# Retention layer of a two-block model: the heads' norm four at a time, and the logarithms of the decays moved into an earlier stage

## The reference

```python
def retention_mixer(...):
    q, k, v, g = split(h @ w_in)         # q, k turned by rope for the latents
    logg = log_sigmoid(decay_logit)      # (2 directions, 8 heads)
    # per head and direction: S_t = exp(logg) * S_{t-1} + k_t v_t^T, y_t = q_t S_t
    y = y_forward + y_backward
    mu, var = mean(y), mean((y - mu)**2) # over the 128 channels of a head
    y = (y - mu) * rsqrt(var + EPS) * gn_g * silu(g)
    return y @ w_out
```

## Time and profile before

| | |
|---|---|
| median of 3 runs | 2895.98 us |
| lowest and highest run | 2881.82, 2899.46 us |
| the profiled execution, its own time | 2883.46 us |
| its span | 2881.5 us |
| busy: TensorE, VectorE, ScalarE | 90%, 42%, 14% of the span |
| products of q | 1309.1 to 1359 us of the span |
| attention stage | 1417.7 to 1565.4 us |
| of that, 1431.5 to 1550: TensorE, VectorE, ScalarE busy | 104.0, 81.9, 45.2 of 118.5 us |
| output projection | from 1565.85 us |

### The profile page before, as it was taken

The page is one execution under the profiler, slowest core; times in us unless marked ns, Lnnn a source line. Parts: engine busy times, 40 slices in busy tenths (PEclk is TensorE's granted clock), DMA queues, the critical chain, the costliest instruction groups (busy, mean ns, idle before and its releaser), DMA issues. The chain is left out here.

```text
span 2881.5 us, 53069 instructions
## 1 busy us (share of the span) xinstructions
PE 2580.2 (90%) x23771; PEld 1817.1 (63%) x23771; DVE 1200.3 (42%) x2046; ACT 417.2 (14%) x925; POOL 240.2 (8%) x219
## 2 busy tenths in 40 slices
PE   7999889589999998999788688888879988899999
PEld 3575675377787564588534564444438666788888
DVE  4635565511111113435767622223235655534452
ACT  2101350200000001100232200000010342110000
POOL 0000000122232210001100110000000300000000
PEclk9999879799999999999899899999999998999999
DMA  7331313689999993215243489999963200222211
GB/s 302 132 127 57 92 34 132 252 330 402 403 400 398 403 404 155 82 44 144 89 139 103 197 350 418 418 418 418 418 279 132 81 15 1 103 88 88 105 68 62
DMA packets 111482, 596.51 MB, mean 207 GB/s; under 512 B 13104, under 2 KB 35568, under 8 KB 47640
## 3 DMA queue, kind: packets, MB, share of 16 engines
q1 hardware_dynamic: 95880, 560.14, 49.2%
q0 software_dynamic: 12000, 22.48, 3.1%
q10 hardware_dynamic: 3376, 10.49, 0.9%
HBM read 572.77 MB, written 16.10 MB: 204 GB/s over the span
## 5 line engine op out<-in xcount | busy, mean ns | idle before, releaser
L1194 PE MATMUL moe_ps<-moe_ring,moe_xs 128*32 128x256 f32 x10240 | 595.9, 382 | 77.1 <-DMA moe_ring<-in_experts 59.8
L1194 PEld LDWEIGHTS moe_ps<-moe_ring,moe_xs 128*32 128x32 f32 x10240 | 393.3, 110 | 278.3 <-DMA moe_ring<-in_experts 83.7
L1194 PE MATMUL moe_ps<-moe_ring,moe_hid_t 128*32 128x256 f32 x5120 | 292.1, 380 | 13.5 <-DMA moe_ring<-in_experts 12.6
L1194 PEld LDWEIGHTS moe_ps<-moe_ring,moe_hid_t 128*32 128x32 f32 x5120 | 193.3, 110 | 113.0 <-DMA moe_ring<-in_experts 25.3
L1433 DVE TENSOR_TENSOR moe_hid<-moe_silu,moe_ps 128x512 f32<-128x512 f32 x32 | 22.0, 688 | 408.1 <-PE moe_ps L1194 398.4
L1394 DVE SCALAR_TENSOR_TENSOR x_feat<-moe_ps,mod,x_feat 128x512 f32<-128x512 f32 (+1 forms) x160 | 104.7, 718 | 122.0 <-PE moe_ps L1268 121.8
L1347 ACT ACTIVATE moe_silu<-moe_ps 128x512 f32<-128x512 f32 x32 | 19.1, 597 | 786.0 <-PE moe_ps L1194 786.0
L1457 DVE TENSOR_SCALAR moe_y<-moe_ps,moe_gates 128x256 f32<-128x256 f32 x42 | 17.8, 478 | 263.7 <-PE moe_ps L1194 263.7
L1225 POOL DMA_INDIRECT moe_rows<-h_rows,moe_rows_id x80 | 77.8, 972 | 476.6 <-DVE moe_xs L1414 363.0
L1235 POOL DMA_INDIRECT acc<-moe_y,moe_rows_id x42 | 66.6, 1586 | 346.0 <-DVE moe_y L1457 337.5
L649 PE MATMUL ffg_ps<-h_feat,feed_f_slots 128*128 128x256 f32 x352 | 82.1, 386 | 1.4 <-DVE h_feat L852 0.9
(11 more groups left out here) (690 smaller groups left out, 3911.7 us busy)
## 6 DMA issues: line engine op xcount, KB each, us to landing
moe_ring<-in_experts SPq DMA_DIRECT2D x384, 1024.0 KB, 27.8
x_feat<-in_ada_w SPq DMA_DIRECT2D x16, 1024.0 KB, 5.3
feed_f_slots<-in_ffn_gate SPq DMA_DIRECT2D x11, 1024.0 KB, 4.9
feed_f_slots<-in_ffn_up SPq DMA_DIRECT2D x11, 1024.0 KB, 5.0
feed_f_slots<-in_ffn_down SPq DMA_DIRECT2D x8, 1408.0 KB, 5.8
gate_rows<-in_ada_w SPq DMA_DIRECT2D x9, 1024.0 KB
qk_ada_w<-in_ada_w SPq DMA_DIRECT2D x8, 1024.0 KB, 4.9
mout_ada_w<-in_ada_w SPq DMA_DIRECT2D x8, 1024.0 KB, 4.7
```

The source lines that it names most:

```text
L1194: mm = pe.matmul(group_ps(part, g)[32 * q:32 * q + 32], turned[:, k * GROUP:(k + 1) * GROUP], ring[:, n % SLOTS, m, q * QUARTER:(q + 1) * ...
```

## The change

`logg` and its helpers move out of the attention stage: the operations on VectorE become `beside["vector"]` of the products of q, the Exp becomes ScalarE's work at the end of its first item. The attention stage waits for the three latent tables first and for the two context tables in head 0 behind its Exp. Two constant tables that the hybrid block also uses are loaded besides: `spread` (64 KB), of which `[:, 2]` has 1/128 in column 0 and zeros in 31 columns, and `back` (192 KB), of which `[:, 0]` has ones in rows 0, 32, 64 and 96.

The squares of four heads are kept in room of `K.h`. In round 5 (and behind the last mix) four products put the means of four heads on rows 0, 32, 64 and 96 of one bank; one root and one reciprocal serve the four heads; for each head a product with `back` spreads its row over all partitions, and VectorE multiplies y by that bank. The spreads of heads 0 to 3 stand before and behind the mixes of rounds 6 and 7, those of heads 4 to 7 at the end, in the four banks `ps_s`.

```diff
--- before.py
+++ after.py
@@ -2158,10 +2158,19 @@
         seven(nc, K, dram, "rv", feed, K.h, halves, evacuate_v, make=False, by_token=True)
 
         latents = K.h[:, :, 0:LAT]
+        logg, la, lb, lc = (sb(n, [P, 16]) for n in ("logg", "la", "lb", "lc"))
+
+        def decays_on_scalar(act, sig, c):
+            if c == 0:
+                log_sigmoid_on_scalar(act, sig, "g", la[:])
+
+        def decays_on_vector(dve, sig):
+            log_sigmoid_on_vector(dve, Steps(dve, sig["logg"]), sig, "g", K.cols("decay_logit", 16), la[:], lb[:], lc[:], logg[:])
+
         with ExitStack() as sub:
             rope = Rope(nc, sub, dram, v)
             seven(nc, K, dram, "rq", feed, latents, tails(K), add_into(q), after=rope.turn_k(k),
-                  beside={"gpsimd": rope.load_k(k)})
+                  beside={"gpsimd": rope.load_k(k), "scalar": decays_on_scalar, "vector": decays_on_vector})
             first, others = silu_behind(g, LAT)
             seven(nc, K, dram, "rg", feed, latents, tails(K), add_into(g), make=False, on_scalar=first, after=rope.turn_q(q),
                   beside={"gpsimd": rope.load_q(q), "scalar": others}, limit=feed.first[4] + 2)
@@ -2176,11 +2185,13 @@
                 tables.append(idle[:, at:at + width])
                 at += width
             later, sooner, once, ctx_f, ctx_b = tables
-            logg, la, lb, lc = (sbs(n, [P, 16]) for n in ("logg", "la", "lb", "lc"))
             lat_w, ctx_w = sbs("lat_w", [P, NL]), sbs("ctx_w", [P, NC])
             ctx_x = sbs("ctx_x", [P, NC])
             prob = sbs("prob", [P, 2, TT, LAT])
-            sq, rstd = sbs("sq", [P, LAT]), sbs("rstd", [P, LAT])
+            rstd = sbs("rstd", [P, LAT])
+            sq = lambda h: K.h[:, 2 * (h % 4):2 * (h % 4) + 2, LAT:TOK]
+            means, back, table = sbs("means", [P, 4, 32]), sbs("back", [P, 3, P]), sbs("table", [P, 1])
+            group = lambda h: slice(32 * (h % 4), 32 * (h % 4) + 32)
             ps_s = sub.enter_context(nc.psum_tensor("ret_pss", [P, 4, 512], F32))
             ps_y = sub.enter_context(nc.psum_tensor("ret_psy", [P, 2, 512], F32))
             ps_n = sub.enter_context(nc.psum_tensor("ret_psn", [P, 512], F32))
@@ -2191,7 +2202,9 @@
                 @block.sync
                 def _(sp):
                     for t, n in ((later, "later"), (sooner, "sooner"), (once, "once"), (ctx_f, "ctx_f"), (ctx_b, "ctx_b")):
-                        sp.dma_start(t, dram[n]).then_inc(sig["tables"], 16)
+                        sp.dma_start(t, dram[n]).then_inc(sig["ctx_tables" if n[0] == "c" else "lat_tables"], 16)
+                    for t, n in ((means, "spread"), (back, "back")):
+                        sp.dma_start(t[:], dram[n]).then_inc(sig["norm_tables"], 16)
                     for m in range(2 * HEADS):
                         side.load(sp, m)
 
@@ -2206,17 +2219,26 @@
                                            start=(j == 0), stop=(j == TT - 1))
                         mm.then_inc(sig["mixed"], 1)
 
-                    def sum_squares(h):
-                        pe.wait_ge(sig["squared"], h + 1)
+                    def sum_squares(first):
+                        pe.wait_ge(sig["norm_tables"], 32)
+                        pe.wait_ge(sig["squared"], first + 4)
+                        if first:
+                            pe.wait_ge(sig["normed"], 4)
+                        for h in range(4):
+                            mm = pe.matmul(ps_n[group(h)], means[:, 2], sq(h), start=True, stop=True, skip_group_check=True)
+                        mm.then_inc(sig["summed"], 1)
+
+                    def spread(h):
+                        pe.wait_ge(sig["inverse"], 1)
                         if h >= 1:
-                            pe.wait_ge(sig["root"], h)
-                        pe.matmul(ps_n[:], K.ones[:], sq[:], start=True, stop=True).then_inc(sig["summed"], 1)
+                            pe.wait_ge(sig["normed"], h)
+                        pe.matmul(ps_n[:], back[group(h), 0], rstd[group(h)], start=True, stop=True).then_inc(sig["spread"], 1)
 
                     for h in range(HEADS):
-                        if h >= 2:
-                            if h % 2 == 0:
-                                side.turn(pe, h // 2 - 1)
-                            sum_squares(h - 2)
+                        if h >= 2 and h % 2 == 0:
+                            side.turn(pe, h // 2 - 1)
+                        if h == 5:
+                            sum_squares(0)
                         for j in range(TT):
                             u = h * TT + j
                             if u >= 4:
@@ -2224,32 +2246,33 @@
                             pe.matmul(ps_s[:, u % 4], k[:, h, j * P:(j + 1) * P], q[:, h], start=True,
                                       stop=True).then_inc(sig["scores"], 1)
                         side.piece(pe, 2 * h)
+                        if h >= 6:
+                            spread(2 * h - 12)
                         if h >= 1:
                             mix(h - 1)
+                        if h >= 6:
+                            spread(2 * h - 11)
                         side.piece(pe, 2 * h + 1)
-                    sum_squares(HEADS - 2)
+                    mix(HEADS - 1)
                     side.turn(pe, HEADS // 2 - 1)
-                    mix(HEADS - 1)
-                    sum_squares(HEADS - 1)
+                    sum_squares(4)
+                    pe.wait_ge(sig["inverse"], 2)
+                    for h in range(4):
+                        pe.matmul(ps_s[:, h], back[group(h), 0], rstd[group(h)], start=True, stop=True).then_inc(sig["spread"], 1)
 
                 @block.scalar
                 def _(act):
-                    log_sigmoid_on_scalar(act, sig, "g", la[:])
-                    act.wait_ge(sig["tables"], 80)
-                    act.wait_ge(sig["logg"], 1)
+                    act.wait_ge(sig["lat_tables"], 48)
 
                     def square(h):
                         act.wait_ge(sig["mixed"], h + 1)
-                        if h >= 1:
-                            act.wait_ge(sig["summed"], h)
-                        act.activation(sq[:], ps_y[:, h % 2], ACT.Square).then_inc(sig["squared"], 1)
-
-                    def root(h):
-                        act.wait_ge(sig["summed"], h + 1)
-                        if h >= 1:
-
-                            act.wait_ge(sig["normed"], h)
-                        act.activation(rstd[:], ps_n[:], ACT.Sqrt, bias=K.col("eps"), scale=1.0 / DV).then_inc(sig["root"], 1)
+                        if h >= 4:
+                            act.wait_ge(sig["summed"], 1)
+                        act.activation(sq(h), ps_y[:, h % 2].rearrange("p (a n) -> p a n", a=2), ACT.Square).then_inc(sig["squared"], 1)
+
+                    def root(n):
+                        act.wait_ge(sig["summed"], n + 1)
+                        act.activation(rstd[:], ps_n[:], ACT.Sqrt, bias=K.col("eps")).then_inc(sig["root"], 1)
 
                     for h in range(HEADS):
                         if h >= 1:
@@ -2257,23 +2280,23 @@
                         act.activation(lat_w[:], later, ACT.Copy, scale=logg[:, h:h + 1]).then_inc(sig["lat_later"], 1)
                         act.wait_ge(sig["lat_log"], h + 1)
                         act.activation(lat_w[:], lat_w[:], ACT.Exp).then_inc(sig["lat_exp"], 1)
+                        if h == 0:
+                            act.wait_ge(sig["ctx_tables"], 32)
                         act.activation(ctx_w[:], ctx_f, ACT.Exp, scale=logg[:, h:h + 1])
                         act.activation(ctx_x[:], ctx_b, ACT.Exp,
                                        scale=logg[:, HEADS + h:HEADS + h + 1]).then_inc(sig["ctx_exp"], 1)
-                        if h >= 2:
-                            root(h - 2)
+                        if h == 5:
+                            root(0)
                         if h >= 1:
                             square(h - 1)
-                    root(HEADS - 2)
+                    act.activation(table[:], K.col("eps"), ACT.Sqrt)
                     square(HEADS - 1)
-                    root(HEADS - 1)
+                    root(1)
 
                 @block.vector
                 def _(dve):
                     step = Steps(dve, sig["dve"])
-                    log_sigmoid_on_vector(dve, step, sig, "g", K.cols("decay_logit", 16), la[:], lb[:], lc[:], logg[:])
-                    dve.sem_inc(sig["logg"], 1)
-                    dve.wait_ge(sig["tables"], 80)
+                    dve.wait_ge(sig["lat_tables"], 48)
 
                     def gate(h):
 
@@ -2283,10 +2306,8 @@
                         dve.sem_inc(sig["copied"], 1)
 
                     def normalise(h):
-                        dve.wait_ge(sig["root"], h + 1)
-                        step(dve.reciprocal(rstd[:], rstd[:]))
-                        step(dve.tensor_tensor(y[:, h], y[:, h], rstd[:], ALU.mult))
-                        dve.sem_inc(sig["normed"], 1)
```

(20 more changed lines are left out.)

## The result

| | before | after |
|---|---|---|
| median of 19 runs each | 2889.28 us | 2901.12 us |
| ratio, 95% interval | | 1.0046 [1.0035, 1.0057], +10.1 to +16.5 us |
| profiled execution, own time | 2883.46 us | 2897.03 us |
| its span | 2881.5 us | 2895.2 us |
| products of q, start to start of those of g | 51.38 us | 53.20 us |

The change makes the kernel slower, by less than 1%. The ratio goes by fast runs alone, which leaves out one run of the kernel before that took 10683 us.

A forecast was written before the change was run, and what follows sets the result against it. It took each head to be bound by a chain from mix through square, Copy, addition, Exp and multiplications to the first weighting. Terms summed to +8.05, say +8.0 us, on 2895.98: 2904.0 us, range 2884 to 2914.

The forecast's parts named there:

- Logarithms in the products of q: Products of q: logarithms ahead of the first combination U delay the first item's fourth product, +1.6 us.
- Tables in two parts: Attention stage's start: the first Copy waits for three tables, not five, and comes earlier, -2.1 us.
- The cover is the wait for the first weighting, which grows by as much: Heads 0 to 3: removed norm work lay beside the chain, so removing it saves only a sliver, -0.1 us.
- Reciprocal behind the gate: Head 5's gate: the four-head reciprocal behind it delays the row copy and head 6's first weighting, +3.25 us.
- spread, +1.0: Head 6: one spread product between the score products and the mix lies on the chain, +1.0 us.
- Spread and `normalise(1)` in head 7: Head 7: a spread ahead of the mix, +1.0 us, and a normalisation behind gate(5) delaying the addition, +0.45 us.
- The end: After the last mix: reciprocal, four side-by-side spreads and four multiplications, 3.78 us against 0.73, +3.05 us.
- Rival C: TensorE's clock halves in the new holes at head 6 (+1.4) and the last spreads (+1.2); 2906.6 us, chance 0.13.
- Its mirror: Output projection: if the last spreads keep the clock up, about 2.4 us come back, 2901.6 us.
- Rivals A, B: Attention heads: VectorE sets the pace, 2883.7 us, chance 0.1; or TensorE sets the pace, 2899.2 us, chance 0.1.
- Rival D: Group products don't run side by side, each set of four costs 2.6 us more; 2908 us, chance 0.07.
- a stage more than 3 us longer than 154.1 us with heads 2 to 5 unchanged: Attention stage in the profile after: would mean a wrong term for heads 5 to 7 or the end.

The follow-up runs named there:

- decays_only: Kernel before with only the logarithms moved into the products of q and the tables waited for in two parts; ratio to before 0.9992.
- one_fill_later: Changed kernel plus one unread product in round 3, where the kernel before had its norm product; ratio to before 1.0049.
- after_filled: Changed kernel plus unread products in TensorE's waits of rounds 2, 3, 4 and 6 and around the last spreads; ratio to before 1.0019.
- norm_only: Changed kernel with the logarithms and the single wait for all five tables back in the attention stage; ratio to before 1.0048.
- recip_hole: Changed kernel with the first four-head reciprocal ahead of the gate instead of behind it; ratio to before 1.0035.
- spread_hole: Changed kernel with that early reciprocal and the spreads of heads 0 and 2 moved into TensorE's wait for a weighting; ratio to before 1.0014.
- after_ahead: Changed kernel with the next head's decay tables built ahead of the previous head's square and gate, and the first reciprocal ahead of the gate; ratio to before 1.0000.
- before_ahead: Kernel before with the next head's decay tables built ahead of the previous head's square and gate; ratio to before 1.0025.

## Why the prediction was right, and where its size was off

The side and the band were right: within 1%, and 2901.12 us lies in the range. The size was not: 8.0 us forecast, 10.1 to 16.5 measured. That 2904.0 lies only 3 us from the measured 2901.12 is luck: the median before was taken from three runs as 2895.98 and came out as 2889.28 over nineteen, 6.7 us lower, which made up for a difference that was forecast some 4 us too small.

- **Logarithms in the products of q, +1.6.** Right: +1.8, in every kernel that has them there.
- **Tables in two parts, -2.1.** Right for the Copy as far as its transfer allowed: 1.5 where that took 5.6 us, 2.1 in `decays_only` where it took the 4.9 of the forecast. The sum lacked what comes behind: the clock returns earlier, and the first mix is 2.9 us sooner in both.
- **"The cover is the wait for the first weighting, which grows by as much", -0.1.** The step that failed. The wait did grow by as much, by 0.9 us. But behind the longer wait of head 3 the clock was at half, which cost 1.7. `one_fill_later` gives it back with one unused product. Head 4's +0.4 is there with the clock full too (16.01 in `after_filled`); `norm_only`, where the logarithms are back in the stage, has 15.66. The trace says where most of it lies: VectorE's addition of the context table begins 0.46 us after the end of ScalarE's second Exp (1496.39 against 1495.93) and not 0.11 as before (1494.99 against 1494.88) and as in `norm_only`. Why is open.
- **Reciprocal behind the gate, +3.25; spread, +1.0.** Right: head 6 without a clock fall is 19.91 - 15.58 = 4.3, and 3.1 of it goes with the reciprocal (16.83 in `recip_hole`).
- **Spread and `normalise(1)` in head 7, +1.45.** Right: +1.6, of which the spread is 1.05 (16.89 to 15.84 in `spread_hole`). A product of the mix takes 0.9. The Trainium skill's page "TensorEngine Tiling (Array Packing)" (Key Properties) says that changing the tiling mode drains TensorE, and gives no time for it. No run here shows a drain by itself; if it is part of a spread's time, it is at most the 0.15 us between 1.05 and 0.9, within the forecast's bound of 0.2.
- **The end, +3.05.** Without a clock fall it is 9.92 - 7.08 = +2.8; with it +3.4 to +3.8.
- **Rival C, 0.13.** Both its falls came, at head 6 (up to +1.2 for a forecast of +1.4) and at the last spreads (+0.6 for +1.2). It was no rival but a part of the likeliest case: of its own condition, "a hole as empty and long as that after 1421.4", the prediction says "it is about as long", and it still got 0.13. It also looked only at the new waits, not at those that a removed product had shortened. Its mirror, 2.4 us back if `rout` began at full clock, did not come in the kernel after, but its size was right: the first two products of `rout` take 4.27 us from start to start of the third in `after_filled`, 6.70 in the kernel before.
- **Rivals A, B.** Neither VectorE nor TensorE set the pace: heads 2 and 5 are unchanged. `after_ahead` shows that the freed VectorE time needs another order to be worth anything.
- **Rival D.** False: eight records in 1.06 us.

With the terms as measured in the heads and the end (1.8 - 2.9 + 1.7 + 0.4 + 5.4 + 1.6 - 0.25 + 3.4) the sum is some 11 us, inside the interval of the runs. The rest of the profiles' 13.7 lies in stages that no edit touches (+1.5 in the products of g, -1.0 ahead of those of q, +2.1 behind the attention stage) and is put down to scatter between executions, with the doubt about g told above. One of the prediction's signs, a stage more than 3 us longer than 154.1 us with heads 2 to 5 unchanged, came by half: the stage took 157.1 us by the same measure (up to the end of VectorE's last multiplication), but 2.1 us of the 3.0 above it lie in heads 3 and 4, which the sign took as unchanged.

## What to carry to other kernels

Work that lies beside the critical path can still carry something: on TensorE, a product in a wait keeps the clock up for what comes behind it. When such a product is removed, or an operation such as a reciprocal makes a new wait, price the next products at half clock too, and look at the granted clock behind every wait that grows, not only behind the new ones. And time freed on an engine that is not the bound is worth nothing until the order of its work is changed to use it; test the new order on the old kernel as well, to see whether the change or the order is what pays.

## What had not been expected of the hardware

- The granted clock fell behind a wait of 2.37 us between stretches in which TensorE was busy (head 3), and did not behind one of 1.45 to 1.51 us in the same place. The records behind it took 3.07 us instead of 1.98.
- Of two waits of 1.8 us in head 7, in the kernel after and in `before_ahead`, the clock fell behind the second and not behind the first.
- Products that nobody reads made the kernel faster: 1.0046 to 1.0019 in the kernel after, `rout`'s first eight records 1.97 us in place of 3.75.
- Work that begins sooner behind a long wait can also meet the full clock sooner: with the first Copy 1.5 us earlier, the first mix came 2.9 us earlier.
